# Ten gather buffers paced by TensorE's pieces, one-hot spills moved from SyncE's queue to GpSimd's, and half of the I one-hots moved from VectorE to ScalarE

## The reference, cut to what matters

```
def peer_ffn(h, wq, keys, u_tab, v_tab):
    ...
    sv, si = lax.top_k(sub, PEER_TOPK)
    ...
    best, pos = lax.top_k(cand, PEER_TOPK)
    experts = jnp.take_along_axis(cid, pos, axis=-1)
    gates = jax.nn.softmax(best, axis=-1)
    ...
        u = jnp.take(u_tab, eb, axis=0)
        act = jax.nn.gelu(jnp.einsum("cd,ced->ce", xb, u))
        vv = jnp.take(v_tab, eb, axis=0)
        return jnp.einsum("ce,ced->cd", gb * act, vv)
```

## Time and profile before

| | us |
|---|---|
| median of 3 runs (1951.26 to 1959.42) | 1957.78 |
| the profiled execution | 1952.49 |
| its span (first to last instruction) | 1950.7 |
| TensorE busy in the span | 1862.3 (95%) |
| VectorE busy | 1580.6 (81%) |
| ScalarE busy | 1031.1 (53%) |
| GpSimd busy | 783.9 (40%) |

### The profile page before, as it was taken

One profiled execution on the slowest core, in us unless ns is written; L12 is line 12 of the kernel. 1 busy time (PEld: TensorE's weight loads), 2 busy tenths in 40 slices (PEclk: granted clock), 3 DMA queues, 4 the chain that ended last, 5 costly groups with the idle time before them and its releaser, 6 DMA issues.

```text
span 1950.7 us, 34571 instructions
## 1 busy us (share of the span) xinstructions
PE 1862.3 (95%) x13106; PEld 1628.1 (83%) x13106; DVE 1580.6 (81%) x2510; ACT 1031.1 (53%) x1868; POOL 783.9 (40%) x686
## 2 busy tenths in 40 slices
PE   8999999999999999999998989988999999999997
PEld 7888887787889888788887877868999999998886
DVE  6768575676534999899987878878988999999998
ACT  5535454474555454666745656535674444444444
POOL 0000000000011113677635677004776777787773
PEclk9999999999999999999999999999999999999999
DMA  7523333246799997888868989977979999999997
GB/s 251 190 86 131 99 99 109 78 133 226 251 302 310 315 321 221 248 265 268 250 216 279 317 283 314 317 249 258 314 246 372 380 387 383 383 393 392 396 382 265
DMA packets 214741, 520.70 MB, mean 267 GB/s; under 512 B 25424, under 2 KB 98416, under 8 KB 214320
## 3 DMA queue, kind: packets, MB, share of 16 engines
q1 hardware_dynamic: 171952, 356.41, 52.9%
q0 software_dynamic: 42624, 162.08, 24.3%
HBM read 472.18 MB, written 46.20 MB: 266 GB/s over the span
## 4 chain that ended last, share of the span: by engine, by line
PE 60%; DMA 14%; DVE 14%; ACT 5%; issue 4%; POOL 3%; SPq 0%; DVEq 0%; ACTq 0%; POOLq 0%
PE ps L2043 59%; DVE lo L1330 4%; DMA raw<-in_peer_u 3%; DMA vraw<-in_peer_v 3%; DMA oneJ_spill<-hspace 2%; DMA hspace<-u_rows,row_ids 1%; POOL u_early L789 1%; PE ps L2447 1%; DMA u_late<-u_rows,row_ids 1%; ACT hi L870 1%; DMA u_early<-u_rows,row_ids 1%; POOL hspace L789 1%; POOL u_late L789 1%; DVE hspace L1862 1%; DMA oneI<-oneI_spill 1%
## 5 line engine op out<-in xcount | busy, mean ns | idle before, releaser
L2043 PE MATMUL ps<-hT,hi 128*128 128x512 f32 x2736 | 990.4, 405 | 39.1 <-DVE lo L1330 38.8
L2043 PE MATMUL ps<-hT,lo 128*128 128x256 f32 x2736 | 769.1, 281 | 0.0
L2043 PEld LDWEIGHTS ps<-hT,hi 128*128 128x128 f32 x2736 | 517.6, 189 | 176.3 <-issue 33.7
L870 ACT ACTIVATE hi<-raw 128x896 fp32r<-128x896 f32 (+1 forms) x406 | 397.2, 991 | 363.8 <-DMA raw<-in_peer_u 303.5
L1330 DVE TENSOR_TENSOR lo<-raw,hi 128x896 fp32r<-128x896 f32 (+1 forms) x406 | 457.6, 1139 | 126.8 <-ACT hi L870 122.5
L2043 PEld LDWEIGHTS ps<-hT,lo 128*128 128x128 f32 x2736 | 520.4, 190 | 0.1
L827 POOL DMA_INDIRECT got<-in_peer_v,row_ids x256 | 345.9, 1351 | 121.9 <-DVE sums L1338 100.9
L1203 ACT ACTIVATE vhi<-vraw 128x896 fp32r<-128x896 f32 (+1 forms) x256 | 193.6, 765 | 255.4 <-DMA vraw<-in_peer_v 247.7
L2043 PE MATMUL ps<-vhi,a_hi 128*128 128x448 f32 x768 | 242.0, 370 | 7.3 <-DVE vlo L1894 5.6
L1338 DVE SCALAR_TENSOR_TENSOR sums<-got,wT,sums 128x704 f32<-128x704 f32 x256 | 243.0, 949 | 1.4 <-DMA got<-in_peer_v,row_ids 0.9
L2043 PE MATMUL ps<-vlo,a_hi 128*128 128x448 f32 x768 | 241.0, 368 | 0.0
(11 more groups left out here) (314 smaller groups left out, 2257.2 us busy)
## 6 DMA issues: line engine op xcount, KB each, us to landing
raw<-in_peer_u SPq DMA_DIRECT2D x256, 448.0 KB, 4.8
vraw<-in_peer_v SPq DMA_DIRECT2D x124, 448.0 KB, 7.9
raw<-in_w_in SPq DMA_DIRECT2D x86, 512.0 KB, 3.4
vraw<-in_peer_v SPq DMA_DIRECT2D x124, 224.0 KB, 8.0
raw<-in_w_out SPq DMA_DIRECT2D x32, 512.0 KB, 3.8
raw<-in_wq SPq DMA_DIRECT2D x32, 512.0 KB, 5.3
turn_in<-in_peer_u SPq DMA_DIRECT2D x32, 512.0 KB, 5.9
u_rows<-turned POOLq DMA_DIRECT2D x32, 512.0 KB, 5.7
```

The costliest lines, as they stand in the source:

```text
L870: nc.scalar.activation(hi[n % NR][:, 0:w], raw[n % NR][:, 0:w], ACT.Copy).then_inc(hi_done, 1)
L2043: return nc.tensor.matmul(o, lhsT, rhs, start=start, stop=stop, skip_group_check=True)
```

## The change

1. **Gathers.** Ten buffers in place of six (`u_buffers` gives each pair its home: `hspace` 0 and 1, `e0` to `e7` in the first half, `l0` to `l3` and `m0` to `m3` in the second, and only six, then four, for the last pairs). The gather of pair k now waits for the dot of pair k - 6 (`dots_made`), for the sums of the pair that had the buffer before, and for TensorE: `mm_done` of the dot's piece less `LEAD` = 6 (one more for the pair's second gather).
2. **Spills.** All 64 pairs of spills leave SyncE's program and stand in GpSimd's, between the gathers, in the order that `pool_order` computes; those from `U_LATE` on behind the last gather.
3. **Late J one-hots** have two buffers: `hspace` (even distance from `U_LATE`) and `tail4` (odd).
4. **I one-hots** of odd groups are made by ScalarE: four `Abs` of 128x128 with bias minus the key (`minus_i`, a new copy at U_FIRST + 2), then one `Relu` of 128x512 (`odd_i`), two pieces after VectorE's J. VectorE makes the others.
5. **The plan.** `pace` grows by 0.92 a piece (was 0.87), odd groups cost 0.75 us (`J_US`), and the search wants the last dot before tile 113. Sums of dots stand three pieces behind the dot (`SUM_LAG`), piece by piece. The rows are now known at tiles 24.5 and 71, the dots stand at tiles 26.5 to 64.5 and 73 to 108, `U_LATE` is 39, and the 25 late groups stand at tiles 109 to 119.5.
6. Two semaphores of an earlier stage are merged into one (`scan_steps`), with the same waits.

```diff
-        pace = min(pace + 0.87, 2.0)
+        pace = min(pace + 0.92, 2.0)
...
+SUM_LAG = 3
+LEAD = 6
...
+    order, key = [], 0.0
+    for k in range(N_PAIR):
+        key = max(key, ROWS_AT[k * NT2 // N_PAIR], DOT_AT[k] - LEAD + 1,
+                  DOT_AT[k - U_BUF] + 0.6 if k >= U_BUF else 0)
+        order.append((key, k, "gather"))
+    order += [(ONE_AT[g] + 0.7, g, "spill") for g in range(U_LATE)]
+    return sorted(order)
...
                     sync.dma_start(raw[n % NR][:, 0:U_PIECE], a["peer_u"][t, half, :, 0:U_PIECE]).then_inc(
                         raw_in[n % NR], 16)
-                    if n - 3 in U_STEPS:
-                        for what, g in U_STEPS[n - 3]:
-                            if what == "one":
-                                spill(g)
...
+            def spill(g):
+
+                split = g >= U_LATE and (g - U_LATE) % 2 == 0
+                pool.wait_ge(sem("madeJ"), g + 1)
+                pool.dma_start(oneJ_dram[g].rearrange("p (a b j) -> p a b j", a=2, b=2) if split else
+                               oneJ_dram[g].rearrange("p (t j) -> p t j", t=TOK4),
+                               made_j(g)).then_inc(sem(f"oneJ_out{g % 3}"), 16)
+                pool.wait_ge(sem("oddI_made" if g % 2 else "madeI"), g // 2 + 1)
+                pool.dma_start(oneI_dram[g].rearrange("p (t i) -> p t i", t=TOK4), made_i(g)).then_inc(
+                    sem(f"oneI_out{g % 2}"), 16)
...
                 if k >= U_BUF:
-                    pool.wait_ge(sem("dots_summed"), k - U_BUF + 1)
+                    pool.wait_ge(sem("dots_made"), k - U_BUF + 1)
+                if U_PREV[k] is not None:
+                    pool.wait_ge(sem("dots_summed"), U_PREV[k] + 1)
...
                 for c in range(2):
+                    pool.wait_ge(mm_done, DOT_AT[k] - LEAD + c)
...
+            def odd_i(g):
...
+                if g >= 3 and g not in (U_LATE, U_LATE + 1):
+                    act.wait_ge(sem("oneI_out1"), 16 * (g // 2))
...
+                for c in range(TOK4):
+                    ins = nc.scalar.activation(made_i(g)[:, c], iota[:, :], ACT.Abs,
+                                               bias=minus_i[:, TOK4 * (g // 2) + c:TOK4 * (g // 2) + c + 1])
+                ins.then_inc(sem("far_made"), 1)
+                act.wait_ge(sem("far_made"), g // 2 + 1)
+                nc.scalar.activation(made_i(g), made_i(g), ACT.Relu, scale=-1.0, bias=one_c).then_inc(
+                    sem("oddI_made"), 1)
...
-                if g > U_LATE:
-                    dve.wait_ge(sem(f"oneJ_out{(g - 1) % 3}"), 16 * ((g - 1) // 3 + 1))
-                elif 3 <= g < U_LATE:
+                if 3 <= g < U_LATE:
                     dve.wait_ge(sem(f"oneJ_out{g % 3}"), 16 * (g // 3))
-                if g < U_LATE:
+                if g >= U_LATE + 2:
+                    dve.wait_ge(sem(f"oneJ_out{(g - 2) % 3}"), 16 * ((g - 2) // 3 + 1))
+                if g < U_LATE or (g - U_LATE) % 2:
...
+                if g % 2:
+                    return
```

More of the change, by code:

```diff
@@ L446, in hybrid_layer_kernel @@
         hspace = at("hspace", [P, 2, KC, SEQ], F32, hT_at)
-        u_early = [ar(f"u_early{i}", 20480 + 512 * i, [P, 2, GATHERED]) for i in range(4)]
-        u_late = [ar(f"u_late{i}", 28672 + 512 * i, [P, 2, GATHERED]) for i in range(4)]
+        u_space = {f"{name}{i}": ar(f"u_{name}{i}", first + 512 * i, [P, 2, GATHERED])
+                   for name, first, n in (("e", 20480, 8), ("m", 26624, 4), ("l", 28672, 4))
+                   for i in range(n)}
+        tail4 = at("tail4", [P, 4, PIECE], F32, raw_at + 4 * (6 * PIECE + U_PIECE))
+        minus_i = at("minus_i", [P, SEQ // 2], F32, end)
         lateI = [at(f"lateI{i}", [P, TOK4, P], BF16, hT_at + 4 * SEQ * (KC + 7 + 8 * i)) for i in range(2)]
@@ L651, in _ @@
                     load_unit(N_Q)
-            for n in range(2 * T_V - 3, 2 * T_V):
-                for what, g in U_STEPS[n]:
-                    if what == "one":
-                        spill(g)
             def load_v(k):
@@ L777, in _, with gather_rows @@
                 pool.wait_ge(sem(f"turn_out{b}"), 16 * (N_UNIT // 2))
-            for k in range(N_PAIR):
+            def spill(g):
[7 more added lines that the diff above has]
+                    sem(f"oneI_out{g % 2}"), 16)
+            def gather_rows(k):
                 t, first = k // (N_PAIR // NT2), 2 * k % PICKS
@@ L793, in _ @@
                         sem(f"got_in{k % U_BUF}"), 16)
+            for _, i, what in pool_order():
+                if what == "gather":
+                    gather_rows(i)
+                else:
+                    spill(i)
+            for g in range(U_LATE, N_TOK4):
+                spill(g)
             def cast_rows(c):
@@ L1156, in dots_sum @@
                 ins.then_inc(sem("dots_summed"), 1)
-            for i in range(N_U):
-                if i < N_U - 1:
-                    hi_piece(2 * (T_U + i) + 2)
-                    hi_piece(2 * (T_U + i) + 3)
+            def odd_i(g):
+                if g == 1:
+                    act.wait_ge(sem("p_made"), 1)
+                    act.wait_ge(freed("idx", 0), PLAN["idx", 0][1] + 1)
+                if g >= 3 and g not in (U_LATE, U_LATE + 1):
+                    act.wait_ge(sem("oneI_out1"), 16 * (g // 2))
+                if g in (U_LATE, U_LATE + 1):
+                    act.wait_ge(sem("dots_summed"), N_PAIR)
+                for c in range(TOK4):
[5 more added lines that the diff above has]
+                    sem("oddI_made"), 1)
+            for i in range(N_U):
+                for n in range(2 * (T_U + i) + 2, 2 * (T_U + i) + 4):
+                    if n < 2 * T_V:
+                        hi_piece(n)
+                    for what, k in U_STEPS.get(n - SUM_LAG, []):
+                        if what == "dot":
+                            dots_sum(k)
+                    for what, g in U_STEPS.get(n - 2, []):
+                        if what == "one" and g % 2:
+                            odd_i(g)
                 if i == 0:
```

71 lines of the change are left out of this document (42 added, 29 removed).

## The result

The changed kernel takes 2001.85 us (median of 4 runs, 2000.91 to 2002.66), against 1958.49 us for the kernel before beside it (4 runs, 1951.26 to 1959.42). The ratio is 1.0229, with an interval of 1.0205 to 1.0253: **slower, by about 45 us**. The forecast was 1969 us with a range up to 1990. The sign is right; the size is not, and the time lies outside the range.

A forecast was written before the change was run, and what follows sets the result against it. The prediction took GpSimd's nearly full queue as the bound in the gather halves and the single J buffer in the late stretch. Terms -3 + 25 + 0 - 9 - 2 = +11 us made 1957.8 into 1969 us, range 1934 to 1990.

The forecast's parts named there:

- The second half, +25: Second half of the gathers: 68 spill DMAs at 0.58 us add 40 us to GpSimd's 190 us queue; +25 us.
- The step that failed: Spills in GpSimd's queue, second half: waits for one-hots and VectorE's waits for landed spills counted as nothing extra.
- what would prove me wrong: Second half: gathers waiting for TensorE (mm_done) would mean GpSimd is not the bound and the +25 us term is wrong.
- the main term: Second half of the gathers: GpSimd's queue, loaded with the spills, is the bound; +25 us, bounds -23 to +56.
- ScalarE's one-hots, 0 (up to +5): Odd I one-hots moved to ScalarE: 1.9 us for each of 32 groups, 61 us, covered by waits; counted 0.
- the sign of a wrong price: Late stretch: waits of ScalarE for oneI_out would show that 0 for the moved I one-hots was wrong.
- The late groups, -9: From tile 108 on: 25 groups at 2.5 us with two J buffers, 106 us against 115 before; -9 us.
- the end, -2: End of the stage: reloads of first_i can start four pieces before the end; -2 us (0 to -4).
- The first half, -3: First half of the gathers, 765 to 1004 us: more buffers shrink 13.8 us of waits; -3 us (-10 to +2).
- (a): Rival, gathers and spills: GpSimd is not the bound, gathers get cheaper; 1944 us, 1921 at the lower bound; chance 0.25.
- (c): Rival, whole sum: losses and gains cancel, +12 in the second half, -2 in all, 1956 us; chance 0.18.
- (b): Rival, late groups: GpSimd's J lands in 5.6 us, 3.2 us a group, loss 26 instead of 8; 1987 us; chance 0.12.

The follow-up runs named there:

- b2: The kernel before plus 68 plain 64 KB DMAs that nobody waits for in GpSimd's program, real spills still by SyncE: 1975.29 us, ratio 1.0091.
- e11: The changed kernel with spills by SyncE and 78 plain DMAs nobody waits for at their old places in GpSimd's program: 1982.68 us, ratio 1.0106.
- e2: The changed kernel with four buffers instead of two for the early I one-hots, spills still by GpSimd: 1987.76 us, ratio 1.0136.
- e10: The changed kernel with four I buffers and all I one-hots made by VectorE: 1981.51 us, ratio 1.0102.
- e4: The changed kernel without pacing, the gathers' waits on mm_done left out: 2023.72 us, ratio 1.0323.
- e1: The changed kernel with the spills issued by SyncE again, all else as changed: 1961.78 us, ratio 0.9999.
- e3: The changed kernel with the I one-hots of odd groups made by VectorE again, spills still by GpSimd: 1990.09 us, ratio 1.0143.
- e5: The changed kernel with spills by SyncE and all I one-hots by VectorE: 1953.41 us, ratio 0.9933.
- e6: The kernel before with a second late J buffer, nothing else changed: 1954.2 us, ratio 0.9956.
- b1: The kernel before with its spills moved into GpSimd's program, placed by the changed kernel's rule: 1997.21 us, ratio 1.0161.

## Why the prediction was wrong, point by point

**The second half, +25: the term was right, the sentence behind it was wrong.** The queue came out at 190 + 43 us where I had 190 + 40, a DMA at 0.58 us where I had 0.58, and the load alone at +18 (b2) and +21 us (e11). The step that failed is this one: "While GpSimd is late these are long done, so I count nothing. ... Both engines are then held by one queue, which is the same term, not a new one." Two engines held by one queue are the same term only if the queue itself never stops. It did stop, for 28 us: 9 for TensorE's piece (`mm_done`), and 14 in two stops for ScalarE's sums (`dots_summed`), the longer one behind a ScalarE that had stood 13 us for a landed spill. GpSimd holds ScalarE and VectorE by a late spill, VectorE holds TensorE, and ScalarE holds GpSimd. With the spills awaited by nobody (e11) or with four I buffers (e2), GpSimd's stops from the first to the last gather were 15 and 9 us instead of 27, and the time between these gathers 248 and 239 us instead of 259. Over the whole kernel e11 puts the waits at 45 - 21 = 24 us (45 - 20 = 25 by e10).

The two programs would have let me see it. The I buffers are two, so the I of a group waits until the spill of the group two before has landed; the plan puts several groups close together, and `pool_order` puts a spill 0.7 of a piece behind its one-hot, but after all gathers with a lower key, eight of them at 1027 us. I costed the load of those 68 DMAs, but not the age of a spill when it is issued: 10 us there, where the kernel before had SyncE issue it beside the gathers.

I had also named what would prove me wrong, gathers that wait for `mm_done` in the second half. They do (10.1 + 1.5 us), and the main term is right all the same. The test confused two statements: GpSimd can be the fullest engine and still not work through. Nor are these waits what closes the ring (e4).

By the Trainium skill, "DMA: Bandwidth & Descriptors", SWDGE vs HWDGE vs iDMA, plain transfers belong to SyncE or ScalarE. The trace agrees, with e1: the same spills by SyncE cost 45 us less. I had weighed it only as a price (0.58 against 0.33 us a DMA).

**ScalarE's one-hots, 0 (up to +5): wrong by 13 to 17 us.** That its own 1.3 + 0.7 us a group cost something, no run shows. The wait in front of them does: ScalarE is in order, and `hi` and the sums stand behind it. e3 gained 17 us, e5 over e1 13 us. With four I buffers the same move was worth 7 us (e10 against e2), and those intervals overlap, so most of the price is probably that wait. I had named waits of ScalarE for `oneI_out` as the sign of a wrong price; they are there, 44.5 us in the second half and 15.8 in the late stretch.

**The late groups, -9, and the end, -2: they came to +4.** VectorE's first use of a reloaded one-hot is 1388.31 - 1335.05 = 53.3 us later than before, tile 108 already 49.4. The end gained its 2 us (a wait of 2.20 became 0.34). A group took 2.9 us, not 2.5. I had looked only at J and its landing. The stretch shows J late by 16.5 us, ScalarE waiting for its I buffer, and GpSimd waiting for ScalarE with the next J behind it:

```profile
POOL oneI_spill L807 <- ACT lateI L1219: 24.9, 11, 3.7
DVE tail L1927 <- DMA oneJ_spill<-tail: 16.5, 10, 3.6
ACT lateI L1215 <- DMA oneI_spill<-lateI: 15.8, 10, 3.2
```

It is the same mistake as in the second half, in small. With SyncE's spills and VectorE's I (e6) the second buffer gave its 9 us.

**The first half, -3: the right sign, and the size agrees by luck.** Tiles 24 to 72 took 242.1 us against 246.2, and tile 72 starts 3 us earlier. GpSimd's waits for the sums are gone (13.8 us before, 0.9 now, with 6.8 us for TensorE's pieces in their place). But b1, b2 and e6 have the first half of the kernel before, and took 253.5, 253.9 and 257.9 us for these tiles, while all nine kernels with ten paced buffers took 240.7 to 245.3. By these the part is worth some 10 us, and the one execution of the kernel before was a fast one. What I didn't see is what the pacing is good for: without it tile 72 starts 26 us later (e4).

**The rivals.** (a) and (c) fell: gathers didn't get cheaper, 1.21 us each (152.6/126) against 1.19. (b) gave the right direction for the late groups: J to J in one buffer took 5.8 us, between my 5 and its 6.4. My range ended at (b) alone; the two mechanisms that decided had no place in it, since both had been declared part of another term.

The sum, by stretches of the two profiled executions: -3 us up to tile 72 (forecast -3), +52 in tiles 72 to 108 (+25), +4 from there to the end of the stage (-11) and -3 behind it (0), so +50 where I had +11. The 39 us between them are 27 + 15 - 3. By the runs, the +52 is 7 us that e1 has too (216.3 against 209.3, hardly more than the scatter of single executions), 27 for the load and 18 for the waits.

## What to carry to other kernels

When an operation moves into another engine's in-order queue, its duration is only one price. Ask how old it will be when it is issued, who waits for its result with how many buffers, and whether that one, by any path, holds the queue itself: if so there is a ring, and no engine's load tells its time. A test with operations that nobody waits for (e11) separates load from waits in one run.
